# Feed-forwards behind a stage make their first chunk tile by tile, with the normed rows stationary and the weights moving

## The reference

```python
y = rmsnorm(x, g)                                   # 256 x 1024
x = x + 0.5 * (silu(y @ w_gate) * (y @ w_up)) @ w_down   # D_FF = 2816, first block
# second block (conv_ffn): u = y @ w_up (gate and value), causal depthwise convolution of
# width 3 over the tokens and a bias, silu(gate) * value, then @ w_down, factor 1
```

## Time and profile before

| | |
|---|---|
| runs, us | 2101.57, 2104.29, 2112.26 (median 2104.29) |
| span of the profiled execution | 2101.1 us |
| PE busy | 2028.2 us, 97% of the span |
| DVE, ACT busy | 1339.4 us (64%), 998.9 us (48%) |
| DMA | 348.94 MB, mean 166 GB/s |

### The profile page before, as it was taken

The page is one execution under the profiler, slowest core; times in us unless marked ns, Lnnn a source line. Parts: engine busy times, 40 slices in busy tenths (PEclk is TensorE's granted clock), DMA queues, the critical chain, the costliest instruction groups (busy, mean ns, idle before and its releaser), DMA issues. The chain is left out here.

```text
span 2101.1 us, 41794 instructions
## 1 busy us (share of the span) xinstructions
PE 2028.2 (97%) x17666; PEld 1877.5 (89%) x17666; DVE 1339.4 (64%) x1985; ACT 998.9 (48%) x1433; POOL 13.0 (1%) x12
## 2 busy tenths in 40 slices
PE   7999999999999999999999989999999999999997
PEld 7999987999999998799989979989998989988997
DVE  6555565754655466575547666577776856577775
ACT  5334456533543345554336544465545544456443
POOL 0000000000000000000000010000000010000000
PEclk9999999999999999999999999999999999999999
DMA  7543731554454362265344324366544333457541
GB/s 301 198 182 111 248 115 77 224 207 162 179 235 184 130 228 81 82 243 206 140 165 173 118 88 142 110 241 235 197 151 151 141 96 112 126 159 272 198 180 51
DMA packets 79878, 348.94 MB, mean 166 GB/s; under 512 B 21232, under 2 KB 30576, under 8 KB 45808
## 3 DMA queue, kind: packets, MB, share of 16 engines
q1 hardware_dynamic: 79728, 346.74, 45.1%
HBM read 345.67 MB, written 1.05 MB: 165 GB/s over the span
## 5 line engine op out<-in xcount | busy, mean ns | idle before, releaser
L89 PE MATMUL bank<-ffn_hT_split,n_split_gate_up 128*128 128x256 f32 x1408 | 391.3, 278 | 2.8 <-DVE ffn_hT_split L199 2.4
L90 PE MATMUL bank<-ffn_hT_split,n_split_gate_up 128*128 128x256 f32 x1408 | 390.7, 277 | 0.0
L91 PE MATMUL bank<-ffn_hT_split,n_split_gate_up 128*128 128x256 f32 x1408 | 390.6, 277 | 0.0
L89 PEld LDWEIGHTS bank<-ffn_hT_split,n_split_gate_up 128*128 128x128 f32 x1408 | 266.1, 189 | 5.2 <-issue 3.6
L90 PEld LDWEIGHTS bank<-ffn_hT_split,n_split_gate_up 128*128 128x128 f32 x1408 | 265.7, 189 | 1.5
L91 PEld LDWEIGHTS bank<-ffn_hT_split,n_split_gate_up 128*128 128x128 f32 x1408 | 265.5, 189 | 0.0
L363 ACT ACTIVATE work<-bank 128x256 f32<-128x256 f32 x88 | 33.3, 383 | 311.2 <-PE bank L91 311.2
L1814 DVE TENSOR_TENSOR mix_parts<-mix_arrived,mix_parts 128x1024 fp32r<-128x1024 f32 x88 | 107.5, 1223 | 93.4 <-ACT mix_parts L1809 93.3
L462 DVE TENSOR_TENSOR work<-bank,work 128x256 f32<-128x256 f32 x88 | 37.2, 423 | 190.2 <-ACT work L363 190.2
L443 DVE TENSOR_TENSOR ffn_split_down<-ffn_arrived_down,ffn_split_down 128x2048 fp32r<-128x2048 f32 x44 | 100.8, 2291 | 81.0 <-ACT ffn_split_down L358 81.0
L426 DVE TENSOR_TENSOR n_split_gate_up<-arrived_gate_up,n_split_gate_up 128x2048 fp32r<-128x2048 f32 x64 | 144.4, 2286 | 9.5 <-ACT n_split_gate_up L348 9.5
(11 more groups left out here) (393 smaller groups left out, 5711.1 us busy)
## 6 DMA issues: line engine op xcount, KB each, us to landing
arrived_gate_up<-in_ffn SPq DMA_DIRECT2D x64, 1024.0 KB, 8.5
ffn_arrived_down<-in_ffn SPq DMA_DIRECT2D x44, 1024.0 KB, 4.8
mix_arrived<-in_mix_w SPq DMA_DIRECT2D x88, 512.0 KB, 3.6
rrived_gate_up<-in_conv_ffn SPq DMA_DIRECT2D x32, 1024.0 KB, 6.8
_arrived_gate_up<-in_ffn SPq DMA_DIRECT2D x24, 1024.0 KB, 6.7
mixer_arrived<-in_w_in SPq DMA_DIRECT2D x22, 1024.0 KB, 7.2
onv_ffn_arrived_down<-in_conv_ffn SPq DMA_DIRECT2D x22, 1024.0 KB, 4.8
irst_project_arrived<-in_w_in SPq DMA_DIRECT2D x17, 1024.0 KB, 4.8
```

The lines of the kernel that those rows point to most:

```text
L89: pe.matmul(out, lhs[0], rhs[0], start=start, stop=False)
L90: pe.matmul(out, lhs[0], rhs[1], start=False, stop=False)
L91: return pe.matmul(out, lhs[1], rhs[0], start=False, stop=stop)
```

## The change

`Phase` gets two hooks that the stage ahead calls: `turn_early` (PE) and `vector_between` (DVE). With them the two blocks of tile 0 are transposed inside the last matmuls of the stage ahead. The first chunk is then made by `hidden_by_rows`: for each token tile, the turned rows (128x128) are stationary and 256 weight columns move. Its rows are copied to SBUF (`copy_rows`) and transposed into the banks in which the rest of the phase expects them (`turn_rows`). The low part of the first up weights is made in four quarters (`low_up`), set between the steps of the norm. `keep_clock` is no longer called for these five phases. In the scan mixer the last three units are taken half by half. The order of the waits and operations of ACT changes with it: `high_down(0, 0)` comes behind `copy_rows(1)`.

```diff
+def turn_block(pe, c, banks, ph, b):
+    t, k0 = b // 2, (b % 2) * 4
+    pe.wait_ge(ph.s["h_ready"], ph.n0["h_ready"] + b + 1)
+    for k in range(k0, k0 + 4):
+        last = pe.transpose(c.ps[banks[b]][:, (k - k0) * P:(k - k0 + 1) * P], c.h[:, t, k * P:(k + 1) * P], c.ident)
+    last.then_inc(ph.s["turned"], 1)
+def turn_tile(pe, c, banks, ph, t):
+    for b in (2 * t, 2 * t + 1):
+        turn_block(pe, c, banks, ph, b)
...
+        def copy_rows(t):
+            act.wait_ge(s["rows_ready"], n0["rows_ready"] + t + 1)
+            act.activation(c.h[:, t, 0:2 * S], c.ps[row_banks[t]][:], ACT.Copy).then_inc(s["rows_copied"], 1)
...
-        for t in range(NT):
-            norm_scalar(act, c, ph, t, ph.prev or ph.start)
-            if ph.prev and t == 0:
-                high_part(0, 0, 16, False, 1)
-        turned_high_scalar(act, c, turn_banks, ph, hT[0])
-        if not ph.prev:
-            high_part(0, 0, 16, False, 1)
-        high_gu(1, 1, 16, False)
+        if ph.prev:
+            norm_scalar(act, c, ph, 0, ph.prev)
+            high_part(0, 0, 16, False, 1)
+            norm_scalar(act, c, ph, 1, ph.prev, lambda: turned_high((0, 1)))   # between the two squares
+            turned_high((2, 3))
+            high_part(1, 1, 16, False, 0)
+            copy_rows(0)
+            high_part(1, 1, 16, False, 1)
+            copy_rows(1)
...
         high_down(0, 0, False)
         step(2, 0, 32, False)
...
+    def low_up(dve, q):
+        dve.wait_ge(s["gu_high"], n0["gu_high"] + 2)
+        ks = slice(2 * q, 2 * q + 2)
...                                   # 128x512 of the low part of up; q == 3 counts for gu_split
+    def vector_between(dve):          # called behind the residual add of (t = 1, half 0)
+        low_up(dve, 0)
+        turned_low(dve, (0, 1))
     def vector_norm(dve, t):
+        if t:
+            low_up(dve, 1)
+            low_up(dve, 2)
         norm_vector(dve, c, ph, t)
...
         if ph.prev:
-            turned_low_vector(dve, c, turn_banks, ph, hT[0], hT[1])
-            low_part(dve, 0, 0, 1)
+            low_up(dve, 3)
+            turned_low(dve, (2, 3))
...
+        def hidden_by_rows():
+            pe.wait_ge(s["gu_split"], n0["gu_split"] + 1)
+            rows(0, 0, range(KT))                 # tile 0, gate: 24 matmuls
+            for q in range(3):
+                pe.wait_ge(s["up_split"], n0["up_split"] + q + 1)
+                rows(0, 1, range(2 * q, 2 * q + 2))   # tile 0, up
+            turn_tile(pe, c, turn_banks, ph, 1)
+            pe.wait_ge(s["gu_split"], n0["gu_split"] + 2)
+            rows(0, 1, range(6, KT))
+            rows(1, 0, range(KT))
+            turn_rows(0)                          # 4 transposes
+            rows(1, 1, range(KT))
...
+            hidden_by_rows()
+            hidden(1, 1, after_first=lambda: turn_rows(1))   # behind the first 24 matmuls
...
         for half in range(2):                    # end of a feed-forward, tile 1
             for f in range(2 if conv is None else 0):
                 down_bank(1, f, 1, half, False, False)
+            if half and ph.nxt:
+                ph.nxt.turn_early(pe)
...
             for k in range(4, KT):               # end of the attention mixer, tile 1
+                if half and k == 6:
+                    ph.nxt.turn_early(pe)
                 out_rows(1, k, half)
...
         for t in range(NT):                      # end of the scan mixer
-            for m in range(N_HALF_UNITS - RING, N_HALF_UNITS):
-                if t == 0:
-                    pe.wait_ge(half_split, ring.split_of(m))
-                out_tile(m, t)
+            for part in range(2):
+                for m in range(N_HALF_UNITS - RING, N_HALF_UNITS):
+                    if t == 0 and part == 0:
+                        pe.wait_ge(half_split, ring.split_of(m))
+                    if t and part and m == N_HALF_UNITS - 1:
+                        ph.nxt.turn_early(pe)
+                    out_tile(m, t, part)
```

More of the change, by code:

```diff
@@ L114, in root_table, with norm_scalar @@
     act.activation(c.stat[:, 7:8], c.eps, ACT.Sqrt)
-def norm_scalar(act, c, ph, t, before=None):
+def norm_scalar(act, c, ph, t, before=None, between=None):
     s, n0 = ph.s, ph.n0
     for half in range(2):
+        if half and between:
+            between()
         n, cols = 2 * t + half, slice(half * D // 2, (half + 1) * D // 2)
@@ L158 @@
 FIRST_BANKS = (0, 1, 2, 3)
+def turn_block(pe, c, banks, ph, b):
[7 more added lines that the diff above has]
+        turn_block(pe, c, banks, ph, b)
 def turn_tensor(pe, c, banks, ph):
     for b in range(2 * NT):
-        t, k0 = b // 2, (b % 2) * 4
-        if ph.prev and t:
+        if ph.prev and b >= 2:
             keep_clock(pe, c, 2 if b % 2 else 9)
[L167 to L170, removed]
+        turn_block(pe, c, banks, ph, b)
     if ph.prev:
@@ L215, in __init__, with turn_early, vector_between @@
             self.s = phase_semaphores(nc, self.stack, phase, names)
+    def turn_early(self, pe):
+        pass
+    def vector_between(self, dve):
+        pass
     def x_ready(self, eng, t, half):
@@ L520, in vector, with turn_early, rows, turn_rows @@
                                          ALU.mult, ALU.add).then_inc(s["residual_done"], 1)
+                if ph.nxt and t and half == 0:
+                    ph.nxt.vector_between(dve)
             if ph.nxt:
                 ph.nxt.vector_norm(dve, t)
+    def turn_early(pe):
+        turn_tile(pe, c, turn_banks, ph, 0)
     def tensor(pe):
+        def rows(t, part, ks):
+            toks = slice(t * P, (t + 1) * P)
+            high, low = w[part][0]
+            for k in ks:
+                if part == 0 and k % 4 == 0:
+                    pe.wait_ge(s["hT_ready"], n0["hT_ready"] + 2 * t + k // 4 + 1)
+                last = matmul3(pe, c.ps[row_banks[t]][:, part * S:(part + 1) * S], (hT[0][:, k, toks], hT[1][:, k, toks]),
+                               (high[:, k, :], low[:, k, :]), k == 0, k == KT - 1)
+            if part and ks.stop == KT:
+                last.then_inc(s["rows_ready"], 1)
+        def turn_rows(t):
+            pe.wait_ge(s["rows_copied"], n0["rows_copied"] + t + 1)
+            for f in range(2):
+                for part in range(2):
+                    last = pe.transpose(c.ps[f][:, part * S + t * P:part * S + (t + 1) * P],
+                                        c.h[:, t, part * S + f * P:part * S + (f + 1) * P], c.ident)
+                if t:
+                    last.then_inc(s["hidden_ready"], 1)
+        def hidden_by_rows():
[10 more added lines that the diff above has]
+            rows(1, 1, range(KT))
         if ph.start:
             ph.start.shared_ready(pe)
-        turn_tensor(pe, c, turn_banks, ph)
-        def hidden(i, slot, first=False):
+        if not ph.prev:
+            turn_tensor(pe, c, turn_banks, ph)
+        def hidden(i, slot, first=False, after_first=None):
             for f in range(2):
```

65 lines of the change are left out of this document (44 added, 21 removed).

## The result

The changed kernel takes 2112.35 us (median of 11 runs, 2107.08 to 2119.12) beside 2103.60 us (median of 11 runs, 2101.57 to 2112.26) for the kernel before: ratio 1.0039, 95% interval 1.0027 to 1.0051. That is 8.2 us slower by the ratio, where 2.45 us were forecast. The profiled spans are 2101.1 and 2111.1 us, mean granted clock 0.995 and 0.991.

A forecast was written before the change was run, and what follows sets the result against it. PE, busy 97% of the span, was taken as the bound, with time to win only at seams between stages. Terms -2.5 - 2.3 + 7.25 = +2.45 us, added to the median, gave 2106.7 us; range for all 2097 to 2113.

The forecast's parts named there:

- The seams: Five stage changes: PE starts the first chunk 4.7 us earlier at feed-forward, 3.4 behind attention, 2.15 behind the scan mixer.
- three first-block seams: Feed-forward to feed-forward and two behind attention: net gain 2.5 us and about 1.15 us each.
- The bound of 0.4 us: First chunk: most that a pitch of 0.118 instead of 0.114 us could cost on its 96 matmuls of 256 columns.
- The wait at conv_ffn's down 0: Late down load delays the product of chunk 0, so PE stalls 3.6 us in each layer, +7.25 us.
- The stall at the 7th of the last matmuls: End of scan mixer: new unit order needs the last unit's low part six matmuls sooner, so PE stalls 1.37 us.
- PEclk 1.00 throughout: Sign that the forecast is right: PE's granted clock stays full everywhere; 0.50 behind a seam would show it wrong.
- the third rival: Clock falls at the seams, 2.8 us a fall: 2112.3 us at two scan seams, 2120.7 at all five; chance 0.10.
- my own main term: The PE stall of 3.6 us at conv_ffn's down 0 in each layer, +7.25 us of the sum.
- The rule of the Trainium skill: Idle gaps between matmul bursts take the clock back to the low level; at the scan seam it would give the third rival's sum.
- the row that I followed instead: Scan seam in the earlier trace, 1403 to 1410: clock stayed 1.00 with 5.73 us of work in 7 us.
- rival 1: Late down load is hidden and the unit order costs nothing: 2097.1 us, or 2093.8 with the shorter pitch; chance 0.22.
- rival 2: Gains of the three seams are lost or equal the scan losses: 2104.3 us, or 2111.5 with full scan stall; chance 0.13.

The follow-up runs named there:

- e1: Changed kernel with the high part of down 0 ahead of the second copy of rows on ACT; PE's wait at down 0 fell from 4.11 to 1.38 us.
- e2: Changed kernel; in conv_ffn's first step silu and product stand ahead of down part 1; 0.66% (13.9 us) under the changed kernel by medians.
- e5: Changed kernel with the scan mixer's last three units taken unit by unit again; 0.20% under the changed kernel.
- e10: Changed kernel with eight keep_clock calls in the projection's first gap; 0.18% under the changed kernel.
- e3: Changed kernel with 15 keep_clock calls filling PE's wait ahead of conv_ffn's down 0; median 0.32% (6.7 us) under the changed kernel.
- e6: Changed kernel with silu and product ahead of down part 1 and the last scan units unit by unit again; 0.45% under the kernel before.
- e7: e6 with eight keep_clock calls in the projection's first gap; median 0.65% under the kernel before.
- e8: e6, but tile 0 is transposed behind the last matmuls of the stage ahead; 0.17% (3.6 us) behind e6 by medians.
- e11: The same kernel as e6 measured again, on one chip with e12; 0.28% under the kernel before.
- e12: The same kernel as e7 measured again, beside e11; median 0.55% under the kernel before.
- e9: Kernel before with eight keep_clock calls in the projection's first gap; 0.14% over the kernel before, interval 0.9997 to 1.0030.
- e4: Changed kernel with conv_ffn and the end of the scan mixer as before, only the first block's three seams new; 0.28% (5.9 us) under the kernel before.

## Why the prediction was right, and where it was not

**The seams: right.** First chunk earlier by 4.72 us (forecast 4.7), 3.09 and 3.44 (3.4), 2.13 and 2.23 (2.15). Net gains of the three first-block seams: 2.73 (2.5), and 0.55 and 1.45 (1.15 each), -4.73 in all against -4.8. The first attention seam falls short of the second by 0.3 us that came up ahead of it and by 0.55 us where I had taken the present pitch for granted: in before the 192 matmuls behind it ran every 0.114 us, and now a part of them runs every 0.118 (48 of them every 0.1174), which gives back 2.54 where the others give back 1.99. The bound of 0.4 us that I had put on it was for 96 matmuls; the slower pitch lasts into the second chunk as well. The four row transposes came cheaper (0.35 instead of 0.44).

**The wait at conv_ffn's down 0: right, in mechanism and size.** The stage starts 3.41 us ahead of before (5.54 less its own 2.13). Shifted by that, after has the high part of down 0 at 1422.01 (forecast 1421.9), the issue at 1426.27 (1426.1), the first chunk at 1408.08 (1408.06) and down 0 at 1436.67 (1436.5): a net of +3.77 and +3.67 us against +3.6. The DMA landed in 4.89 us where 4.88 were taken from the earlier trace rows. e1 moves the load and e2 leaves it and moves what stands behind it; both take the wait away, which shows the chain link by link. The stall at the 7th of the last matmuls was 1.50 us from start to start, so 1.27 beyond the pitch of 0.23 (1.37 forecast).

**"PEclk 1.00 throughout": wrong; this is the step that failed.** I priced the third rival at the seam's small pieces (1.4, 1.1, 0.3 us), found the longest at 1.4 us and gave it 0.10. I had not put my own main term to the same question: the wait that I forecast at down 0 is 3.6 us of idle PE, as long as the 3.73 us of the earlier trace rows, behind which the earlier trace rows show 0.50. I named 1.4 us as "the longest single piece" in the same text that forecasts 3.6. The measured wait brought a granted clock of 0.50 in 6 of 6 profiled passes (after, e5, e10, two each), none where the wait was filled (e3), cut to 1.4 us or less (e1) or gone (e2, e6, e7, e8, e11, e12). The cost was 1.41 and 2.88 us in after, 4.3 together, where 2.8 a fall had been the third rival's price. Two falls on top of my sum are the 2112.3 us that stood there with a chance of 0.10, beside 2112.35 measured; so close an agreement is partly luck, by the next point. The rule of the Trainium skill, "TensorE: Matmul & The Clock Gate", section "Why this matters for your kernels", which I weighed and set aside, held for this wait; the row that I followed instead (5.73 us of work in 7) spoke of small pieces only. For the pieces of the seam itself it was right in after, where the clock held at 1.00, but not a safe rule: of the 20 passes over the new scan seam in after, e1, e2, e3, e5, e6, e7, e10, e11 and e12 the clock fell at it in 2, layer 2 of e5 and of e11, and in e8, where one piece had grown to 2.00 us, in both. So the third rival names something real that after happened to be spared.

**Not forecast, and not shown to be the change's own: 3.3 us.** The projection of both layers was 1.66 and 1.61 us longer, with the clock falling at a gap that before has too. The 8 of 20 above say that this comes and goes in nearly the same program, so it belongs to the profiled pair and perhaps only in part to the medians. Whether the change makes such falls likelier is open: before was profiled without the filler in two passes only, and e10 against e9 does not settle it. The 0.60 us in front of the projection come and go as well: in e1, e5, e8 and e11 the low stretch there is as long as in before, and the gain is nothing. By the terms shown, -4.7 + 7.4 + 4.3 = +7.0 us are the change's own in this pair of profiles; the interval of the ratio (5.7 to 10.7 us) holds that, but the 1.95 us between e9 and e10 do not fit it, and no run tells why.

**The rivals.** The load was not hidden (rival 1); the gains of the three seams were not lost (rival 2, against which e4 stands). The range held the time near its upper end, and the sign, faster or slower, was the forecast's. But a 2.45 us term inside the noise and an 8.2 us slowdown are not the same answer.

## What to carry to other kernels

A preparation step that is put behind a late wait takes with it every DMA that waits for its buffer: move the one instruction that frees the buffer ahead of the wait (e1), or put what the bottleneck needs ahead of what the next load needs (e2). Whenever a forecast contains a new idle stretch of the matmul engine, compare that stretch itself with the gaps that already lowered the clock in the trace, and add the price of the slow matmuls to the price of the wait. And price every idle stretch by all the gaps in the trace, not by the one that first catches the eye: a gap of 2.2 us lowered the clock here too. Changes in one program can be kept seam by seam: the parts that gain here (three seams, 0.28%) were hidden under one part that lost.

## What the runs showed of the hardware

- A gap of 2.1 us between starts (1112.09 and 1114.21) is enough for the clock to fall, sometimes: 8 of 20 passes, against 6 of 6 behind the waits of 3.7 to 4.5 us at down 0. A wait of 2.00 us with one of 1.44 ahead of it did it in both layers of e8. I had expected only pieces of about 3.7 us to matter. The trace of before could have told me: PE is idle for 2.24 and 2.26 us in the attention mixers of both layers, and the granted clock is 0.50 behind both. In all fourteen profiles that is so in 24 of 28 passes. The first of them in before, and the window behind it:

```profile
325.74 0.47 PE L89 MATMUL bank<-mixer_parts,mixer_T_parts 128*128 128x512 f32 x1 [2.24 <-issue]
```
```profile
328.00:330.00 2.00, 2.00 (x26) 1.35 (x27) 0.00 (x0) 0.56 (x3) 0.00 (x0) 0.50 0.00 0
```

- The length of a fall varies: about 3 us at the projection's gap, 3 to 7 us at down 0 and in front of the projection, almost 14 us once in e9 and once in e10.
- A second, smaller step in the speed of matmuls, with the granted clock at 1.00: 256 columns every 0.1135 us or every 0.118, and in down 0 of before's conv_ffn 512 columns every 0.233 instead of 0.229, so some 0.0045 us each at both widths. In e1's conv_ffn of layer 1 the matmuls of 256 columns kept the slow pitch for nine chunks (those of 512 hardly, 0.2296), 0.42 us a chunk, 3.8 us in all; most of what e1 lacks against e2 may be this. The first down matmul of two neighbouring chunks, first in before (16.40 us apart), then in e1 (16.82). No run told its cause.

```profile
1449.40 0.39 PE L89 MATMUL bank<-conv_ffn_split_down,conv_ffn_act_split 128*128 128x512 f32 x1
...
1465.80 0.39 PE L89 MATMUL bank<-conv_ffn_split_down,conv_ffn_act_split 128*128 128x512 f32 x1
```
```profile
1445.09 0.40 PE L89 MATMUL bank<-conv_ffn_split_down,conv_ffn_act_split 128*128 128x512 f32 x1
...
1461.91 0.40 PE L89 MATMUL bank<-conv_ffn_split_down,conv_ffn_act_split 128*128 128x512 f32 x1
```
